# First expert's up products behind its gate products, and its down product ahead of the second expert, in a one-core decoder step with 32 experts

## The reference, cut to what matters

```
def hier_moe(h, rg_w, rg_b, re_w, re_b, w_gate, w_up, w_down):
    t = h.reshape(n * l, d)
    g_top, g_idx = lax.top_k(softmax(t @ rg_w + rg_b), 1)         # 1 of 4 groups
    e_top, e_idx = lax.top_k(softmax(logits of that group), 2)    # 2 of its 8 experts
    combine = one_hot(eid, 32) * gate
    hid = silu(t @ w_gate[e]) * (t @ w_up[e])                     # 1024 -> 256
    y = (hid * combine) @ w_down[e]                               # 256 -> 1024
```

## Time and profile before

| | us |
|---|---|
| median of 3 runs | 692.66 |
| lowest, highest | 689.54, 694.28 |
| the profiled execution, its own time | 692.57 |
| its span in the profile | 690.8 |
| PE busy, share of the span | 658.1 (95%) |
| DVE busy | 575.2 (83%) |
| ACT busy | 408.5 (59%) |

### The profile page before, as it was taken

The page is one execution under the profiler, slowest core; times in us unless marked ns, Lnnn a source line. Parts: engine busy times, 40 slices in busy tenths (PEclk is TensorE's granted clock), DMA queues, the critical chain, the costliest instruction groups (busy, mean ns, idle before and its releaser), DMA issues.

```text
span 690.8 us, 11414 instructions
## 1 busy us (share of the span) xinstructions
PE 658.1 (95%) x3970; PEld 567.8 (82%) x3970; DVE 575.2 (83%) x808; ACT 408.5 (59%) x521; POOL 248.6 (36%) x182
## 2 busy tenths in 40 slices
PE   8999999998999999997999999999999999998996
PEld 5999999998998889846878888888878777766885
DVE  5599999987776474476899999999999999968785
ACT  7331322236262132375699999999999889862322
POOL 1151498979429230004233333333334343310001
PEclk9999999999999999997999999999999999999999
DMA  9651331121039272627489999999999999775211
GB/s 291 201 153 32 129 117 62 62 86 49 1 99 317 77 243 101 234 110 248 173 353 381 374 374 378 367 378 394 394 390 377 379 377 371 292 290 188 77 61 62
DMA packets 49532, 156.10 MB, mean 226 GB/s; under 512 B 6938, under 2 KB 28634, under 8 KB 36427
## 3 DMA queue, kind: packets, MB, share of 16 engines
q1 hardware_dynamic: 35905, 133.98, 51.6%
q10 hardware_dynamic: 9346, 12.13, 5.3%
q0 software_dynamic: 4240, 9.44, 3.8%
HBM read 143.55 MB, written 17.59 MB: 233 GB/s over the span
## 4 chain that ended last, share of the span: by engine, by line
PE 66%; DVE 11%; DMA 9%; issue 6%; ACT 4%; POOL 2%; ACTq 0%; SPq 0%; POOLq 0%; DVEq 0%
PE bank L606 62%; DMA ring<-in_w_expert_up 4%; PE bank L610 4%; DMA ring<-in_w_expert_down 2%; DMA out<-front 2%; ACT catT_parts L2037 1%; DVE front L1777 1%; DVE ring_parts L1445 1%; DVE front L1778 1%; DMA uext<-expert_rows 1%; DVE z L1412 1%; DVE front L1804 1%; POOL z L2403 1%; DMA scratch<-h_rows,sorted_tok 1%; POOL grs L2396 1%
## 5 line engine op out<-in xcount | busy, mean ns | idle before, releaser
L1445 DVE TENSOR_TENSOR ring_parts<-ring,catT_parts 128x2048 fp32r<-128x2048 f32 x64 | 143.6, 2281 | 0.0
L2037 ACT ACTIVATE catT_parts<-ring 128x2048 fp32r<-128x2048 f32 x64 | 122.6, 1916 | 9.1 <-PE bank L606 6.0
L606 PE MATMUL bank<-ring_parts,hT_high 128*128 128x256 f32 (+1 forms) x748 | 113.7, 296 | 0.0
L2449 POOL DMA_INDIRECT expert_rows<-scratch,cur_code x32 | 47.5, 1485 | 181.2 <-issue 126.2
L606 PEld LDWEIGHTS bank<-ring_parts,hT_high 128*128 128x128 f32 x748 | 100.6, 189 | 4.0 <-DVE ring_parts L1315 0.2
L1284 DVE SCALAR_TENSOR_TENSOR bank<-uext,cpar,bank 128x512 f32<-128x512 f32 x116 | 86.0, 741 | 0.0
L1634 DVE TENSOR_TENSOR ring_parts<-ring,down_high 128x2048 fp32r<-128x2048 f32 x30 | 68.8, 2294 | 7.7 <-ACT down_high L2142 6.2
L2296 POOL TENSOR_TENSOR ring_parts<-ring,ring_parts 128x2048 fp32r<-128x2048 f32 x11 | 51.7, 4702 | 58.6 <-ACT ring_parts L1852 58.6
L606 PE MATMUL bank<-ring_parts,catT_parts 128*128 128x256 f32 (+1 forms) x360 | 67.3, 324 | 2.5 <-DVE front_parts L1341 1.3
L606 PE MATMUL bank<-catT_parts,xT_odd 128*128 128x512 f32 x256 | 65.8, 400 | 1.5 <-ACT catT_parts L2037 1.5
L606 PEld LDWEIGHTS bank<-ring_parts,catT_parts 128*128 128x128 f32 x360 | 54.6, 191 | 8.9 <-issue 1.7
(11 more groups left out here) (342 smaller groups left out, 1281.4 us busy)
## 6 DMA issues: line engine op xcount, KB each, us to landing
ring<-in_w_expert_gate SPq DMA_DIRECT2D x32, 1024.0 KB, 5.5
ring<-in_w_expert_up SPq DMA_DIRECT2D x32, 1024.0 KB, 7.5
ring<-in_w_expert_down SPq DMA_DIRECT2D x32, 1024.0 KB, 8.1
ring<-in_w_in SPq DMA_DIRECT2D x12, 1024.0 KB, 7.0
ring<-in_w_out SPq DMA_DIRECT2D x4, 1024.0 KB, 5.0
ring<-in_w_ple_gate SPq DMA_DIRECT2D x4, 1024.0 KB, 7.5
catT<-in_x_prompt SPq DMA_DIRECT2D x4, 512.0 KB, 4.9
z<-in_x_prompt SPq DMA_DIRECT2D x4, 512.0 KB, 5.5
```

Of the source, the lines that this page charges most:

```text
L606: return nc.tensor.matmul(out, lhsT, rhs, start=start, stop=stop, skip_group_check=True)
L1445: V.tensor_tensor(ring_r[:, 3 * par + m, :], ring[:, 3 * par + m, :], cat_r[:, m * CHUNK:(m + 1) * CHUNK].bitcast(F32), ALU.subtract).then ...
L2037: A.activation(cat_r[:, m * CHUNK:(m + 1) * CHUNK], ring[:, s, :], ACT.Copy).then_inc(S["w_hi"], 1)
L2449: G.indirect_dma_start(moe_d, bass.IndirectOffsetOnAxis(ap=cur_code[0:r, par:par + 1], axis=0), yout[0:r, par, :], None, bounds_check=2 * ...
```

## The change

PE does the first expert's up products directly behind its gate products, then the slot table, then all eight remaining tiles without a break, with the transpose of the first expert's hidden values behind tile 4. Then comes the first expert's down product, and only then the second expert's three passes (without the transpose between them). The loop begins with expert 2.

ACT copies the second expert's up weights ahead of the first silu (it stood behind tile 3), does the silu only when gate and up are both done (it needed gate alone), then copies tiles 1 to 5 in a row and the transposed hidden values behind tile 5 (they stood behind tile 8). Its first step no longer has that copy.

DVE does the product of the first expert's hidden values and the slot codes ahead of tiles 1 to 6. Before, tiles 1 to 3 came ahead of the hidden values, and the slot codes behind all tiles.

```
@@ tensor engine
             sorted_T(0)
-            gate_up_first((0,))
+            gate_up_first((0, 1))
             table(slotone, blockone, NBLK, 4)
-            for t in range(1, 4):
+            for t in range(1, NT):
                 sorted_T(t)
-            gate_up_first((1,))
-            for t in range(4, NT):
-                sorted_T(t)
-            for q in range(1, NX):
+                if t == 4:
+                    hid_T(0, 0)
+            down_plain(0, 0)
+            gate_up(0, 1, 0)
+            gate_up(0, 1, 1)
+            for q in range(2, NX):
                 step(0, q)
@@ vector engine
-            for t in range(1, 4):
-                sorted_half(t)
             w_low(0, 1, 0)
             second = window_begin(0, 1)
             hidden(0, 0)
-            for t in range(4, 7):
+            slot_codes()
+            for t in range(1, 7):
                 sorted_half(t)
             x_low(0, 1, second)
             for t in range(7, NT):
                 sorted_half(t)
             w_low(0, 1, 1)
-            slot_codes()
@@ scalar engine, silu
-                if isinstance(i, int) and i == 0 and par == 0:
-                    act.wait_ge(S["ga_done"], 1)
-                else:
-                    act.wait_ge(S["gu_done"], 2 * i + par + 1)
+                act.wait_ge(S["gu_done"], 2 * i + par + 1)
@@ scalar engine, step
                 if plain(*before(i, q)):
-                    hid_plain(*before(i, q))
+                    if not first:
+                        hid_plain(*before(i, q))
@@ scalar engine, before the loop
             second = window_begin(0, 1)
+            w_high_part(0, 1, 1)
             silu(0, 0)
-            for t in range(1, 4):
+            for t in range(1, 6):
                 sorted_half(t)
-            w_high_part(0, 1, 1)
-            for t in range(4, 6):
-                sorted_half(t)
+            hid_plain(0, 0)
             act.wait_ge(S["xs_act"], 6)
             act.wait_ge(S["xs_dve"], 6)
             x_out(0, 1, second)
```

## The result

The changed kernel took 697.35 us in the median of 4 runs (693.2 to 701.45), the kernel before 691.1 us in 4 runs; the ratio is 1.0094, with a 95% interval of 1.0049 to 1.014. It is slower, by 0.3 to 1.4%, and 696.7 had been forecast. The profiled execution was the quickest of the four: 693.2 us, with a span of 691.3.

What follows compares the result with a forecast made beforehand. PE was taken to bound the kernel. Terms 0.5 + 0.65 + 0.9 - 0.55 + 0.4 + 2.55 - 0.35 = 4.1 us on the profiled 692.57 gave 696.7 us, 0.6% slower, range 692.5 to 701.

Steps and rivals of the forecast that it cites:

- What bounds: From tile 0 on, PE ends last; what it loses ahead of the loop is kept to the end.
- The hole: Ahead of the third expert's first pass, PE waits for ACT's gate copy, silu and up copy: +2.55 us (2.0 to 2.8).
- The waits among the tiles: Tiles 1 to 8: tile 3 waits for DVE +0.65, tile 8 for ACT +0.9, replacing an old wait, -0.55 us.
- still in front of ACT's release of tile 8: Tile 7's gather, 5.0 to 6.0 us long, lands up to 1 us late but before ACT frees tile 8's banks.
- stage 2: First expert's down product waits for tile 7 from DVE, whose low window stands ahead of it: +0.4 us (0 to 1.3).
- The clock in the up products: First expert's up products, now behind gate, run their first 0.87 us at the low clock: 3.4 us, +0.5.
- The sum: All terms together: third step's hidden transposes 4.1 us later, at 352.2 instead of 348.11; 696.7 us, 0.6% slower.
- signs named for being right or wrong: Right: tile 8 waits for ACT, PE about 2.5 us for ACT's catT copy; wrong: clock under 1.00 between 326 and 355.
- Only the hole: Rival, chance 0.13: waits at two tiles and ahead of the down product vanish; 2.1 or 1.6 us, 694.2 to 694.7.
- Late loads absorb it: Rival, chance 0.07: in the loop's last third, loads running on their own swallow the 4.1 us; 692.6 or a little under.
- The hole costs the clock: Rival, chance 0.12: PE's idle stretch ahead of the third expert drops the clock, 2.8 us more, 699.5.
- The clock falling among the transposes: Rival, chance 0.06: during eight tiles of only transposes the clock falls, +6 to +7 us, 703 to 704.

Runs made afterwards that it cites:

- both sets of the changed kernel: The unedited changed kernel against the kernel before, measured twice: first 4 runs, ratio 1.0094; second 12 runs, with a second profile, ratio 1.0065.
- the down product back: Changed kernel with the first expert's down product moved back behind the second expert's products: ratio 1.0009 to the kernel before.
- the run with the loads late: Changed kernel with SP's expert 2 gate and up loads held until tile 8 is gathered: ratio 1.0079; same edit on the kernel before: 0.9982.
- the run with the clock kept: Kernel before with 36 instead of 14 products that nobody reads ahead of tile 0: ratio 1.0006 to the kernel before.
- the run with the longer hole: Changed kernel with ACT copying the third expert's gate weights twice and 34 unread products on PE ahead of its first pass: ratio 1.0124.
- filling the hole: Changed kernel with 18 products that nobody reads on PE ahead of the third expert's first pass: ratio 1.0069 to the kernel before.
- down product ahead alone: Kernel before with only the first expert's down product, and what it needs, moved ahead of the second expert: ratio 1.0105.

## Why the prediction was right

**What bounds.** Right in the main. PE's lateness at the third expert is still there 21 steps on (4.2 of 4.3 us), both sets of the changed kernel are slower, with intervals that leave out 1, and the down product back gives the time back. That the last part of the loop, with its late loads, keeps all of it is not shown.

**The hole.** Forecast 2.55, measured 2.36 as idle time in every profile with it and 2.53 from start to start, for the reason given: gate copy, silu, up copy on ACT, of which only the last pass is covered. It is the largest term.

**The waits among the tiles.** The sum was nearly right, one releaser was not. Forecast were 0.65 for tile 3 (measured 0.49), 0.9 for tile 8 by ACT, 0.4 ahead of the down product: 1.95 together. Measured: 0.49, 1.32 for tile 7's gather, 0.3 for tile 8's, and 0.25 ahead of the down product (336.80 - 335.66 - 0.9), 2.4. The step that failed is "still in front of ACT's release of tile 8". The gather of tile 7 did land in front of it, but by 0.3 us only (334.40; ACT had tile 6 out at 334.71), and tile 8 cannot start before tile 7 has been transposed and its own gather, which the forecast left out, has landed (335.61). The second profile, in which the clock came back only during the up products, shows the same: tile 7 waited 1.07 for its gather. The bounds of 5.0 to 6.0 us for a gather were those of one profile; in the changed kernel's first profile one took 9.8. The sum held all the same, because the down product hung on DVE's low window and its copy of tile 7, as forecast for stage 2, and that came when the gathers were early, too (the run with the loads late).

**The clock in the up products.** The +0.5 was not found: in the profiled execution the clock was back at 322.4, before up began, and up took 2.85 us (325.91 - 323.06); in the second profile it took 3.03 (330.64 - 327.61), against 2.93 in the kernel before. Where the clock rises differs by execution, in both kernels, so this is hardly a term of the change.

**The sum.** The hidden transposes of the third step were to come 4.1 us later. From gate's end they come at 23.3 and 23.1 us in the two profiles of the kernel before (348.11 and 346.98), at 27.4 in the changed kernel's second profile (355.01): 4.1 and 4.3 later. The first profile has 0.35 more through the fallen clock. That the sum fits to 0.2 us is in part luck: the 0.5 for up is in it and was not there, and the waits among the tiles, measured at 0.4 more, made up for it. Of the signs named for being right or wrong, tile 8 did not wait for ACT, and the clock was under 1.00 between 326 and 355 us in the first profile (0.50 in 350 to 352), a cost that the sum does not have.

**The rivals.** Only the hole: no, the tiles' waits are there. Late loads absorb it: not all of it, since both sets of the changed kernel are slower; a part is open. The hole costs the clock: it happened in the changed kernel's first profile and in the one with loads late, not in two others with the same 2.36 us; where it happened it cost 1.5 us in two passes, less than the 2.8 forecast, since the clock was back before 354 us (1.00 in 354 to 356). (The 6.2 us from which the 2.8 were worked out begin at 319.56; tile 0, at 316.44, had run at the low clock too.) The Trainium skill's rule on idle gaps ("TensorE: Matmul & The Clock Gate", "Why this matters for your kernels"), which the prediction holds against the hole, is worded for longer gaps than this one. The clock falling among the transposes: not in the changed kernel's profiles (1.00 in 330 to 332, where PE did nothing else).

The Trainium skill ("TensorE: Matmul & The Clock Gate", "Part 4: PE-mode transpose") says that the full clock does not engage in transposes; these rows speak against it. Tiles did run at the low clock, but in these profiles only behind longer waits for a gather: tile 0 in two profiles of the kernel before (1.94 us behind 3.00, and behind 2.70 in the one with loads late), tile 8 in the run with the clock kept (behind 1.93), and tiles 7 and 8 in the run with the longer hole (behind 2.29). In that last one the clock fell behind the wait and was back as the down product began, with nothing but the transposes of these two tiles in between:

```profile
338.00:340.00 2.00, 1.00 (x5) 1.00 (x6) 1.22 (x1) 0.29 (x1) 0.00 (x0) 0.77 0.12 41
340.00:342.00 2.00, 2.00 (x11) 2.00 (x10) 0.69 (x1) 0.60 (x1) 0.00 (x0) 0.50 0.00 0
342.00:344.00 2.00, 2.00 (x8) 1.26 (x7) 1.30 (x2) 1.03 (x2) 0.00 (x0) 0.87 0.00 0
```

**The size.** The first set's ratio means 3.4 to 9.7 us, the second's 2.4 to 6.6; 4.1 lies in both. What part of the rest is the clock's, and what is chance of the loads, stays open: filling the hole did not tell them apart. The loads' part is not small: from the transposes of the third step to the last ones the loop took 256.9 us in one profile (hole longer) and 264.8 in another (down product ahead alone), and between 257.5 and 260.9 in the two profiles of the kernel before.

## What to carry to other kernels

A product that seems to stand late may be the work that covers another engine's row of copies: before moving it, list what that engine has to do between the last read of a shared buffer and the next use, and what covers that. A wait among several limits that lie close together is not won by removing one of them; the sum of the stage has to be worked out again with the next releaser. And where an execution's early part moves with the clock, compare two profiles from a point behind it.

## What was not expected of the hardware

The idle gap ahead of tile 0, about 2.6 to 3.0 us in both kernels, brought the clock down at different places: before tile 0 in the first profile of the kernel before (its stretch from 314 to 316 at 0.87), and only behind tile 0 in the changed kernel's (1.00 there, 0.50 in 320 to 322). Gate's 24 matmuls took from 4.3 to 5.3 us for that reason alone, in kernels whose TensorE does the same up to there.

The same hole of 2.36 us left the clock up in two profiles and took it down in two.
